# Hybrid trunk, float32, one core: the opening loads of c, the small vectors, B and C on other queues and in another order

## What is computed

```python
c_act = silu(c)
for l in range(2):
    mod = c_act @ w_mod[l] + b_mod[l]
    sh1, sc1, g1, sh2, sc2, g2 = split(mod, 6)
    h = rmsnorm(x, norm1_g[l]) * (1 + sc1) + sh1
    q, k, v, ca, cb, su, gates = split(h @ w_in[l])
...
    x = x + g1 * (mixed @ w_out[l])
    h2 = rmsnorm(x, norm2_g[l]) * (1 + sc2) + sh2
    x = x + g2 * ((silu(f_gate) * f_up) @ w_ffn_out[l])
return rmsnorm(x, final_norm_g)
```

## Time and profile before

| | |
|---|---|
| median of 3 runs | 1221.28 us |
| lowest, highest | 1218.03, 1222.57 us |
| span of the profiled execution, first to last instruction | 1215.0 us |
| around the span, to the median | 6.3 us |
| TensorE (matmuls) busy | 84% |
| DVE, ScalarE, GpSimd busy | 66%, 38%, 28% |
| mean granted TensorE clock | 0.912 |
| DMA | 193.78 MB, mean 159 GB/s |

### The profile page before, as it was taken

How to read it: one execution, slowest core, us unless ns; L and a number is a source line. 1 busy time by engine, 2 the same in 40 slices (tenths; PEclk the granted TensorE clock), 3 DMA queues, 4 the chain that set the end, 5 groups by cost and what they waited for, 6 DMA issues and landing times.

```text
span 1215.0 us, 17787 instructions
## 1 busy us (share of the span) xinstructions
PE 1015.0 (84%) x7606; PEld 916.0 (75%) x7606; DVE 798.1 (66%) x1026; ACT 463.8 (38%) x504; POOL 341.5 (28%) x76
## 2 busy tenths in 40 slices
PE   0777668886878889999998877877687988999998
PEld 0375557775767879999997766776585887999998
DVE  0468987998983546545455689899898434544544
ACT  0444363433223445445544223442331434434432
POOL 0143334461545530000003424446154663000000
PEclk9786988897889989999998979889788998999999
DMA  9721423563346656676677314544343444555540
GB/s 313 208 89 51 173 70 107 170 208 113 131 174 187 213 182 228 219 265 220 214 272 173 105 35 139 139 139 139 104 139 133 145 141 134 177 176 192 188 139 36
DMA packets 144544, 193.78 MB, mean 159 GB/s; under 512 B 30611, under 2 KB 123667, under 8 KB 138321
## 3 DMA queue, kind: packets, MB, share of 16 engines
q1 hardware_dynamic: 138272, 190.66, 47.5%
q10 hardware_dynamic: 6192, 1.97, 0.7%
HBM read 191.57 MB, written 1.05 MB: 159 GB/s over the span
## 4 chain that ended last, share of the span: by engine, by line
PE 54%; DVE 31%; issue 7%; ACT 4%; ACTq 2%; DMA 1%; SPq 1%; DVEq 0%
PE bank L451 15%; PE bank L452 14%; PE bank L453 14%; DVE yc L1327 10%; PE bank L487 3%; DVE m L1299 2%; PE bank L550 2%; DVE prod L1303 2%; DVE m L1294 2%; DVE h L1369 2%; ACTq L367 1%; PE bank L513 1%; DVE m L1291 1%; DVE m L1292 1%; PE bank L533 1%
## 5 line engine op out<-in xcount | busy, mean ns | idle before, releaser
L817 POOL TENSOR_TENSOR wlo<-raw,whi 128x2048 fp32r<-128x2048 f32 x72 | 341.3, 4740 | 683.4 <-PE bank L453 538.1
L451 PE MATMUL bank<-hhi,whi 128*128 128x256 f32 x1504 | 455.6, 303 | 27.8 <-DVE hlo L1228 12.4
L452 PE MATMUL bank<-hlo,whi 128*128 128x256 f32 x1504 | 443.6, 295 | 0.0
L453 PE MATMUL bank<-hhi,wlo 128*128 128x256 f32 x1504 | 442.5, 294 | 0.0
L451 PEld LDWEIGHTS bank<-hhi,whi 128*128 128x128 f32 x1504 | 306.9, 204 | 60.2 <-issue 46.4
L837 ACT ACTIVATE whi<-raw 128x2048 fp32r<-128x2048 f32 x132 | 251.8, 1908 | 173.4 <-DMA raw<-in_w_in 49.2
L452 PEld LDWEIGHTS bank<-hlo,whi 128*128 128x128 f32 x1504 | 307.4, 204 | 0.3
L453 PEld LDWEIGHTS bank<-hhi,wlo 128*128 128x128 f32 x1504 | 305.9, 203 | 0.0
L1106 DVE TENSOR_TENSOR wlo<-raw,whi 128x2048 fp32r<-128x2048 f32 x60 | 137.5, 2292 | 166.6 <-PE bank L453 117.0
L451 PE MATMUL bank<-bhi,whi 128*128 128x256 f32 x608 | 179.5, 295 | 29.5 <-DVE h L1365 8.9
L453 PE MATMUL bank<-bhi,wlo 128*128 128x256 f32 x608 | 177.0, 291 | 0.0
(11 more groups left out here) (206 smaller groups left out, 880.8 us busy)
## 6 DMA issues: line engine op xcount, KB each, us to landing
raw<-in_w_mod SPq DMA_DIRECT2D x44, 1024.0 KB, 7.3
raw<-in_w_ffn_in SPq DMA_DIRECT2D x44, 1024.0 KB, 5.1
raw<-in_w_in SPq DMA_DIRECT2D x38, 1024.0 KB, 5.9
raw<-in_w_ffn_out SPq DMA_DIRECT2D x22, 1024.0 KB, 5.0
raw<-in_w_out SPq DMA_DIRECT2D x8, 1024.0 KB, 6.8
raw<-in_w_in SPq DMA_DIRECT2D x16, 256.0 KB, 5.1
raw<-in_w_attn_o SPq DMA_DIRECT2D x8, 512.0 KB, 7.0
raw<-in_conv_pw_w SPq DMA_DIRECT2D x4, 1024.0 KB, 5.2
```

The costliest lines, as they stand in the source:

```text
L451: mm(o, w_hi, a_hi, start=start, stop=False, skip_group_check=True)
L452: mm(o, w_hi, a_lo, start=False, stop=False, skip_group_check=True)
L453: return mm(o, w_lo, a_hi, start=False, stop=stop, skip_group_check=True)
L817: nc.gpsimd.tensor_tensor(wlo[mi % N_LO][:, :], raw[SLOT[("main", l, i)]][:, :], whi[mi % N_HI][:, :].bitcast(F32), ALU.subtract).then_inc ...
```

## The change

c gets a load of its own, the very first on SyncE's queue, into another part of a free tile, and is turned by a transpose of its own; ScalarE takes the silu straight from PSUM. `rows` shrinks to 120 rows and the small loads to 12. For layer 0 they are issued by ScalarE right behind the silu, and TensorE turns them behind block 0 of w_mod. `prep(0)` goes behind ScalarE's copies of x. The late constants and B and C of layer 0 are issued by GpSimd, and each layer has its own semaphore for B and C.

```diff
@@ names and tiles @@
+VROWS = R_FIN + DK
-N_ROWS = 13
+N_ROWS = 12
-        rows = prod[1][:, 0, 0:P]
+        rows = prod[1][0:VROWS, 0, 0:P]
+        crow = prod[1][0:DK, 2, 0:P]
-        vec = [sb(f"vec{l}", [P, P]) for l in range(DEPTH)]
+        vec = [sb(f"vec{l}", [P, VROWS]) for l in range(DEPTH)]
+        s_c, s_const, s_const2, s_x = sem("c_landed"), sem("const_landed"), sem("late_const_landed"), sem("x_landed")
+        c_tr = sem("c_tr")
+        s_bc = [sem(f"bc_landed{l}") for l in range(DEPTH)]
@@ small_vectors @@
-            eng.dma_start(rows[R_C:R_C + DK, :], A["c"].rearrange("b (r c) -> (b r) c", c=P)).then_inc(s_rows[l], 16)
@@ sync @@
+            sp.dma_start(crow, A["c"].rearrange("b (r c) -> (b r) c", c=P)).then_inc(s_c, 16)
             sp.dma_start(ident[:, :], A["c_ident"]).then_inc(s_const, 16)
...
-                if n == 1:
-                    small_vectors(sp, 0)
@@ tensor @@
             pe.wait_ge(s_const, 32)
-            small_columns(0)
+            pe.wait_ge(s_c, 16)
+            nc.tensor.transpose(b_mod[:, 0:DK], crow, ident[0:DK, 0:DK]).then_inc(c_tr, 1)
             for k in range(DK):
                 mod_block(0, 0, k)
+                if k == 0:
+                    small_columns(0)
@@ gpsimd @@
+            late_constants(pool)
+            b_and_c(pool, 0)
@@ scalar @@
             load_x(act)
-            late_constants(act)
-            b_and_c(act, 0)
-            act.wait_ge(vec_cp, 1)
-            fn(cact[:, :], vec[0][:, R_C:R_C + DK], ACT.Silu).then_inc(silu_c, 1)
-            prep(0)
+            act.wait_ge(c_tr, 1)
+            fn(cact[:, :], b_mod[:, 0:DK], ACT.Silu).then_inc(silu_c, 1)
+            small_vectors(act, 0)
             for n in range(4):
                 act.wait_ge(x_tr, n + 1)
                 fn(x[:, 2 * n:2 * n + 2, :], halves(bank[4 + n][:, :]), ACT.Copy).then_inc(x_cp, 1)
+            prep(0)
             norm(0)
@@ vector @@
-                dve.wait_ge(s_bc, 64 * (l + 1))
+                dve.wait_ge(s_bc[l], 64)
...
-            small_vectors_in(0)
             dve.wait_ge(silu_c, 1)
             V.tensor_copy(cact32[:, :, :], bcast(cact[:, :], 32)).then_inc(c_ready, 1)
+            small_vectors_in(0)
             discretize(0)
             b_factor(0)
```

More of the change, by code:

```diff
@@ L64 @@
 C3 = float(np.float32(TWO_PI - C1 - C2))
-R_BMOD, R_N1, R_N2, R_DWB, R_LNG, R_LNB, R_D, R_ARE, R_AIM, R_FIN, R_C = 0, 48, 56, 64, 68, 72, 76, 80, 96, 112, 120
+R_BMOD, R_N1, R_N2, R_DWB, R_LNG, R_LNB, R_D, R_ARE, R_AIM, R_FIN = 0, 48, 56, 64, 68, 72, 76, 80, 96, 112
+VROWS = R_FIN + DK
 M_SH1, M_SC1, M_G1, M_SH2, M_SC2, M_G2 = 0, 8, 16, 24, 32, 40
@@ L295, in trunk @@
         posi = modrow[:, 0:T].bitcast(I32)
-        s_const, s_const2, s_bc, s_x = sem("const_landed"), sem("late_const_landed"), sem("bc_landed"), sem("x_landed")
+        s_c, s_const, s_const2, s_x = sem("c_landed"), sem("const_landed"), sem("late_const_landed"), sem("x_landed")
+        c_tr = sem("c_tr")
+        s_bc = [sem(f"bc_landed{l}") for l in range(DEPTH)]
         s_rows = [sem(f"rows_landed{l}") for l in range(DEPTH)]
@@ L364, in b_and_c @@
             for c, name in enumerate(("ssm_b_re", "ssm_b_im")):
-                eng.dma_start(bn[:, c], A[name][l].rearrange("g n i -> (g n) i").rearrange("(s p) i -> p s i", p=P)).then_inc(s_bc, 16)
+                eng.dma_start(bn[:, c], A[name][l].rearrange("g n i -> (g n) i").rearrange("(s p) i -> p s i", p=P)).then_inc(s_bc[l], 16)
             for c, name in enumerate(("ssm_c_re", "ssm_c_im")):
-                eng.dma_start(cn[:, c], A[name][l].rearrange("g o n -> (g o) n").rearrange("(s p) n -> p s n", p=P)).then_inc(s_bc, 16)
+                eng.dma_start(cn[:, c], A[name][l].rearrange("g o n -> (g o) n").rearrange("(s p) n -> p s n", p=P)).then_inc(s_bc[l], 16)
         def load_x(eng):
@@ L714, in small_columns @@
                     pe.wait_ge(h_ready, H_PER_LAYER * l)
-                nc.tensor.transpose(b_y[:, 0:P], rows, ident[:, :])
+                nc.tensor.transpose(b_y[:, 0:VROWS], rows, ident[0:VROWS, 0:VROWS])
                 nc.tensor.transpose(b_y[:, P:P + ST], ldtr, ident[0:ST, 0:ST])
@@ L1414, in small_vectors_in @@
                 dve.wait_ge(vec_tr, l + 1)
-                V.tensor_copy(vec[l][:, :], b_y[:, 0:P])
+                V.tensor_copy(vec[l][:, :], b_y[:, 0:VROWS])
                 V.tensor_copy(ldv[l][:, :], b_y[:, P:P + ST])
```

## The result

| | before | after |
|---|---|---|
| median | 1222.59 us (1217.99 to 1227.39, 16 runs) | 1228.15 us (1226.50 to 1234.59, 16 runs) |
| ratio, 95% interval | | 1.0056 (1.0039 to 1.0074) |
| span of the profiled execution | 1215.0 us | 1225.8 us |
| its own time | not given | 1227.64 us |
| mean granted TensorE clock | 0.912 | 0.913 |

The changed kernel is 5.6 us (0.45%) slower by the medians and 0.56% by the ratio on record, which is not the quotient of the medians. That it is slower is clear from the interval; whether by more than 0.5%, what can be told from no change, is not. The forecast was 1224, with 1211 to 1238.

What follows compares the result with a forecast made beforehand. It took TensorE's opening to be bound by loads sharing DMA turns, one packet per queue. T 29.6 + 24.9 put the row's copy at 54.5 instead of 51.69, so 1215.0 + 2.8 + 6.3 gave 1224 us, range 1211 to 1238.

Steps and rivals of the forecast that it cites:

- main case: Opening: TensorE's gap moves behind block 0, small loads share turns with w_mod, row's copy 2.8 us later; chance 0.50.
- T: Start of DVE's copy of ssm_log_dt, once the small loads are in: 29.6 us, against 15.49 before.
- q10 and q1 with equal counts of packets from 8 us on: Sign in the DMA windows: ScalarE's queue (q10) and SyncE's (q1) start equally many packets from 8 us on.
- squares, mean square: TensorE, behind prep(0): 4.48 us, the duration of before (36.95 to 41.43).
- row's copy: Copy of the modulation row, end of the opening: starts at T + 24.9 = 54.5 us instead of 51.69.
- around the span: Time outside the profiled span: median 1221.28 less 1215.0, 6.3 us.
- GpSimd's packets come in between as a third queue: Opening, while the small loads come in: 40 packets of GpSimd's constants, mostly 512-byte rows, add 1.7 us to T.
- upper bound of 34: High end for T, if all of B and C (320 pieces on each engine, 4 us) also come first.
- GpSimd's loads hidden: B and C on GpSimd's queue: landed at 38 us, last moment 46, so hidden by 8 us.
- Rival B: GpSimd's queue is the wait: 5120 pieces at 10 ns, in at about 58 us, total 1236 us; chance 0.20.
- Rival A: Opening: TensorE's gap goes, small loads not held to equal turns, T 15.7 to 19.1, total 1210.2 to 1213.6; chance 0.22.
- Rival C: Opening: queues' turns only partly equal, T 21 to 27 or so, total 1215 to 1222 us; chance 0.08.

Runs made afterwards that it cites:

- e1: After with conv_dw_w loaded in two DMAs (16 and 15 rows) instead of one: 1219.77 us, ratio to before 0.9984.
- e5: After with GpSimd waiting for the 12 small loads before it issues late constants, B and C: 1225.96 us, ratio to before 1.0019.
- e3: After with prep(0) back ahead of ScalarE's copies of x: 1224.23 us, ratio to before 1.0003.
- e6: Before with only late constants, B and C of layer 0 issued by GpSimd: 1215.59 us, ratio to before 0.9920.
- e8: e6 with GpSimd waiting for the 13 small loads before its own: 1212.24 us, ratio to before 0.9899.
- e9: After with the small loads on SyncE's queue behind w_mod block 0 and prep(0) ahead of x's copies: 1214.18 us, ratio to before 0.9913.
- e2: After with the 12 small loads on SyncE's queue behind w_mod block 0: 1215.62 us, ratio to before 0.9941.
- e4: After with conv_dw_w alone on SyncE's queue behind w_mod block 0: 1217.82 us, ratio to before 0.9954.
- e7: After with small loads ahead of w_mod on SyncE, conv_dw_w split, small columns and prep(0) earlier, GpSimd waiting, block 7 before w_in: 1207.93 us, ratio to before 0.9880.
- e10: e7 with the modulation row's copy ahead of the split of the first w_in: 1206.21 us, ratio to before 0.9859.

## Why the prediction was right, and where it was off

**Direction and mechanism were right.** The main case said that the gap on TensorE moves behind block 0 instead of going, that one packet a turn is the reason, that conv_dw_w sits on one engine, and that prep(0) is laid bare. The gap of after ends when the small loads are in (33.06) and block 1 starts at 34.45; conv_dw_w is DVE's releaser; 28 of q10's packets stand in 10 us, and e1 takes 9 us away by splitting that load; and from L890's table load to the squares (40.16 to 43.76) there are 3.60 us, the predicted number. 1228.15 lies inside the range and inside the likeliest case's own (1219 to 1229). T, 33.06, is past the 32.8 from which the prediction counted its main case as slower (0.12); within 0.5% had the higher chance, and the ratio came out at 1.0056, at that edge.

One of its signs wasn't seen: "q10 and q1 with equal counts of packets from 8 us on". From 8 to 18 us there are 169 and 282, and in e5, without a third queue, 243 and 560. Small loads don't keep a row waiting on all 16 engines, as B's pieces did; equal turns can hold only on the engines that have rows of both, and there they are argued from the times.

**Step by step** (forecast, measured in the chain of after):

| term | forecast | measured |
|---|---|---|
| silu | 6.1 | 6.65 |
| block 0 used by | 11 | 10.73 |
| T | 29.6 | 33.06 |
| ldt's copy, transposes | 1.47 | 1.46 |
| block 1 | 1.82 | 1.87 |
| transposes of x, copies | 3.25 | 3.77 |
| prep(0) | 3.60 | 3.60 |
| squares, mean square | 4.48 | 6.57 |
| blocks 3 to 7 up to the row | 10.26 | 11.15 |
| row's copy | 54.5 | 61.48 |
| around the span | 6.3 | 1.84 |

**The step that failed first is "GpSimd's packets come in between as a third queue: 40 of its constants, mostly 512-byte rows, 1.7 us".** It measured 5.7 (after less e5). The count without GpSimd was not the error: it came out at 27.9 against 27.32. For GpSimd I took 40 turns at some 0.04 us. Its whole queue, B and C included, has 384 packets, 24 for each DMA engine on average, so these are fewer turns at 5.7 / 24 = 0.24 us each (an estimate from these counts). I took the row size of the other two queues for GpSimd's, where its large packets are 4.1 KB, and I had nothing for what they do to w_mod's rows (0.42 us each instead of 0.28, e5 above). T stayed under the upper bound of 34, but that bound was mis-worked: 320 pieces on each of 16 engines at 2329 pieces in 4 us are 8.8 us and not 4, which gives 38; the same text uses this rate rightly for B and C (8.4 us for 304).

**The second is the mean square**, 5.90 us on TensorE instead of the 3.70 of before, which the forecast carried over. It isn't more work; the granted clock is lower under it. TensorE's windows of before, then of after (window, busy, PEclk, DMA share, GB/s):

```profile
36.00:41.40 5.40, 4.81 (x46) 1.00 1.15 338
41.40:43.00 1.60, 1.60 (x13) 0.54 1.35 218
```

```profile
39.40:44.40 5.00, 1.05 (x9) 1.00 1.34 220
44.40:46.00 1.60, 1.57 (x13) 0.87 1.34 217
46.00:50.30 4.30, 4.30 (x25) 0.50 0.37 60
50.30:53.00 2.70, 2.70 (x17) 0.50 0.00 0
```

Before, the full clock (2.4 GHz) held until the mean square was done at 41.4 us, and the low level (1.2 GHz) fell on the blocks behind it. After, it falls 1.6 us into the mean square, and from 46 us on all of it runs at 0.50. Why it falls there is open. The idle 4 us ahead of the mean square are not needed for it: e3 takes them away, and the clock falls in it as well (TensorE, windows of e3):

```profile
41.00:42.50 1.50, 1.47 (x14) 1.00 1.23 208
42.50:44.00 1.50, 1.50 (x11) 0.57 1.34 228
44.00:46.50 2.50, 2.50 (x16) 0.50 1.34 217
```

The kernels whose silu of c comes behind the small loads (before, e6, e8), so that blocks 0 and 1 run without a gap, have 3.70, 4.21 and 4.02 us for it; all those with c first (the other nine) 5.12 to 6.96. e9 and e6, which differ in c's own load and what hangs on it, have 5.36 and 4.21. That is a pattern of twelve kernels and not a mechanism.

**Smaller ones.** The transposes of x with their copies took 0.5 us more than in before, the blocks behind the mean square 0.9 more, of which the low clock up to 53 us is a part. Together: T +3.5, the steps behind it +3.5, so 61.48 for 54.5.

**"What lies around the span, 6.3 us" was no such thing.** It is 1.84. I had set the span of one execution against the median of others, and that execution was a short one. The forecast was 1215.0 + 2.8 + 6.3 = 1224.1. Measured is 1215.0 + 9.8 (row's copy) + 1.0 (behind it) + 1.84 + 0.5 (own time to median) = 1228.15. An opening too short by 7 us and a surround too long by 4.5 partly cancel, so the closeness of the two medians is partly luck; for the difference to before I said +2.8 and the medians have +5.6.

**GpSimd's loads hidden: right, with more room.** The timeline of GpSimd's queue, and then, from the DMA window 4 to 12.5 us, two of its loads with KB and us from issue to landing:

```profile
4.07 1.17 POOL L368 DMA_DIRECT2D yc<-in_ssm_b_re  x1
5.23 1.15 POOL L368 DMA_DIRECT2D yc<-in_ssm_b_im  x1
6.38 0.76 POOL L370 DMA_DIRECT2D yc<-in_ssm_c_re  x1
7.13 0.75 POOL L370 DMA_DIRECT2D yc<-in_ssm_c_im  x1
```

```profile
yc<-in_ssm_b_re POOLq DMA_DIRECT2D x1, 128.0 KB, 9.7
...
yc<-in_ssm_c_im POOLq DMA_DIRECT2D x1, 128.0 KB, 12.1
```

The last is in at 7.13 + 12.1 = 19.2 us; I had said 38, and 46 for the last moment. The low bound for an issue was nearer (0.54 to 1.17 us measured). The same large packets that held the small loads up brought B and C in early, so one mis-sized term was wrong on both sides. Rival B, with its 7.8 ns a piece, is out: the two issues of B, 2048 pieces each, took 1.17 and 1.15 us. By the Trainium skill's fit ("DMA: Bandwidth & Descriptors", Anatomy of one DMA) an estimate is 2.3 us for each 128 KB and 21 us for all nine one after another; the trace has them in 18 us after the first issue at 1.25. A single one took 9.7 to 12.1 us beside w_mod, far more than the fit has for one.

**Rival A** (T under 19.1) is what e2 and e6 reach, with the loads on the other queue: 18.76 and 18.79. For T = 19.1 it had the row's copy at 44.0; e2 has 47.66, e6, with prep(0) first, 43.84. Its condition wasn't met. **Rival C** (21 to 27) is where e1 and e4 are, by other edits.

**What the change is worth by its parts** (ratios against before, each with an interval of some 0.2% either way). GpSimd's part alone is a gain of 0.8% (e6), 1.0% if its loads wait for the small ones (e8). c first is worth nothing (e9 against e6). The small loads behind the silu on ScalarE's queue cost 1.15% (e2, 0.9941, against after, 1.0056), of which splitting conv_dw_w gives back 0.7% (e1). The place of prep(0) costs 0.5% (e3). The prediction added up one path and gave no part a worth of its own, so it didn't say that one part of this change is a gain by itself and another eats it.

## What to carry to other kernels

A first load that starts the critical engine early is worth only what that engine can do before its next wait: follow the path to the second thing it needs. Small loads that are wanted before a stream of large rows are better placed on that stream's own queue, ahead of it (T 8.87 in e7, against 33.06); on another queue they share turns with the large rows, and a load whose rows all fall to one DMA engine pays a turn for each row, so give such a load a row count that spreads (16 + 15 instead of 31: 9 us here). Before adding a third queue ask how large its packets are and what they do to the rows beside them, not only how many they are; and set one profiled execution against its own time, not against a median of others.

## What the runs showed that I had not expected

**The size of a packet depends on the queue.** 4096 pieces of 64 bytes and more were 384 packets on GpSimd's queue (0.93 MB), where ScalarE's had 2329 packets for 0.33 MB. GpSimd's queue so moves small pieces well, and slows the others down: w_mod got 282 rows in 10 us instead of 560, each lasting half as long again.

**conv_dw_w's 31 rows go to one engine**, 16 and 15 do not. The views don't name the engine; it is read from the pace of 0.36 us a row and from e1. The Trainium skill ("DMA: Bandwidth & Descriptors", Why a DMA increments its semaphore by 16 and not by 1) says that the engines used are the largest number up to 16 that divides the slowest dimension: 1 for 31, 16 for 16, 15 for 15. The trace of e1 agrees: T 23.94 instead of 33.06.

**A split on GpSimd holds some instructions of DVE.** In e10 the first hlo, which reads h and hhi, both in SBUF, took 3.86 us instead of 0.47 and ended 0.3 us behind GpSimd's first split, while the three h ahead of it, which read x from SBUF and a bank of PSUM, took 1.26 together, the later ones beside the split (timeline of e10; the hlo stands above). A later hlo took 4.46 us beside the second split (49.49 to 54.02):

```profile
41.63 1.26 DVE L1230 SCALAR_TENSOR_TENSOR h<-x,scale,bank 128x256 f32<-128x256 f32 x3 [0.81 <-PE bank L524]
41.89 4.50 POOL L826 TENSOR_TENSOR wlo<-raw,whi 128x2048 fp32r<-128x2048 f32 x1 [26.30 <-ACT whi L846]
```

The kernel before has the same thing in small, beside its first split of 51.77 to 56.28; this instruction on 8 columns should take some 0.2 us, as its neighbour L1201 does:

```profile
54.13 0.18 DVE L1201 TENSOR_TENSOR modv<-bank,vec 128x16 f32<-128x16 f32 x1 [4.61 <-PE bank L495]
54.35 1.95 DVE L1206 SCALAR_TENSOR_TENSOR scale<-modv,vec 128x8 f32<-128x8 f32 x1
```

The Trainium skill ("GPSIMD Engine Reference", 1. Specifications) says that GpSimd shares its SBUF interfaces with DVE, and that instructions of DVE with two inputs from SBUF contend; the rows agree: hlo and L1206 read two, h and L1201 one. In e10 little is to be had from it, since the third main matmul wants the split's own result at 47.39 us. Moving the split to another engine wasn't tried.

**Executions of one kernel differ by some us.** e2's row of modulation is 4.0 us earlier than before's, its median 8.5 us lower, and yet its profiled span is the same 1215.0. ScalarE's copies of the main blocks are 6.3 us ahead of before's at 302 us and 1.2 ahead at 339, level from 800 us on. TensorE's windows of before, then of e2:

```profile
294.00:324.00 30.00, 24.38 (x177) 0.89 0.41 147
```

```profile
294.00:324.00 30.00, 18.83 (x128) 0.85 0.49 172
```

The clock can be the result of the waiting here as well as its cause, and the two windows are not the same work, since e2 is 6 us ahead. Most profiles of the experiments have such a loss, those of after and e7 don't. The ratios carry something of it: all eleven come out 2 to 6 us lower than the offset of the row's copy against before's 51.69 says (e1: 0.3 us later, ratio 0.9984; e4: 0.6 us later, 0.9954). A ratio of two of these kernels so tells more on the opening than a ratio against before. And a profiled span says little on a few us in the whole, and the offset of the same instruction in the opening says more.
